# Seven block products for each branch's gates, with weight sums made by adding transfers and by VectorE

## The reference, cut to what matters

```
mod = silu(c) @ ada_w + ada_b -> shift_m, scale_m, gate_m, shift_f, scale_f, gate_f   (6 x 1024)
h = rms_norm(x) * (1 + scale_m) + shift_m
proj = h @ w_in     -> inputs of four mixers (pool, spatial gating, conv, attention), and gate_cols (256 x 4096)
branch[n] = y_n @ w_branch[n]                       n = 0..3, each (256 x 256) @ (256 x 1024)
merged = sum over n of sigmoid(gate_cols[n]) * branch[n]
x = x + gate_m * (merged @ w_out)
h2 = rms_norm(x) * (1 + scale_f) + shift_f
route each token to 6 of 64 experts; x = x + gate_f * (experts(h2) + shared(h2))
out = rms_norm(x)
```

## Time and profile before

| | us |
|---|---|
| median of three runs | 766.91 |
| the profiled execution's own time | 767.08 |
| its span, first to last instruction | 765.3 |
| TensorE busy | 724.8 (95%) |
| VectorE busy | 333.1 (44%) |
| ScalarE busy | 171.4 (22%) |
| GpSimd busy | 35.7 (5%) |
| bytes moved by DMA | 271.43 MB |

### The profile page before, as it was taken

The page is one execution under the profiler, slowest core; times in us unless marked ns, Lnnn a source line. Parts: engine busy times, 40 slices in busy tenths (PEclk is TensorE's granted clock), DMA queues, the critical chain, the costliest instruction groups (busy, mean ns, idle before and its releaser), DMA issues.

```text
span 765.3 us, 11751 instructions
## 1 busy us (share of the span) xinstructions
PE 724.8 (95%) x4678; PEld 320.0 (42%) x4678; DVE 333.1 (44%) x793; ACT 171.4 (22%) x345; POOL 35.7 (5%) x30
## 2 busy tenths in 40 slices
PE   4899999999999999999999999999999997999894
PEld 1588854444444444343343433433333342333231
DVE  1108695979743485333234332331333332322234
ACT  3213332000001333222122221221222221212113
POOL 0200001223130000000000000000000000000000
PEclk9999999999999999999999999999999999999997
DMA  9999617968668398999999999999999999999992
GB/s 341 378 352 389 199 51 275 366 213 326 252 243 361 133 382 285 394 415 419 406 400 421 421 419 417 412 421 420 420 421 420 412 417 421 420 422 420 415 402 87
DMA packets 67204, 271.43 MB, mean 355 GB/s; under 512 B 4984, under 2 KB 13312, under 8 KB 46544
## 3 DMA queue, kind: packets, MB, share of 16 engines
q1 hardware_dynamic: 65584, 264.78, 87.4%
q0 software_dynamic: 1264, 5.79, 2.0%
q10 hardware_dynamic: 304, 0.13, 0.1%
HBM read 269.62 MB, written 1.05 MB: 354 GB/s over the span
## 4 chain that ended last, share of the span: by engine, by line
PE 73%; DMA 19%; SPq 3%; DVE 2%; ACT 1%; issue 1%; POOLq 0%; ACTq 0%; DVEq 0%
PE bank L1198 71%; DMA ring<-exp_w_dram 16%; DMA ring<-w_in_dram 2%; SPq L375 2%; SPq L378 2%; PE bank L1586 1%; DMA reg<-reg 1%; PE bank L1388 0%; DVE bank L1151 0%; DVE reg L1031 0%; PE bank L1287 0%; POOLq L116 0%; ACT L650 0%; ACT h_hT L675 0%; ACT reg L549 0%
## 5 line engine op out<-in xcount | busy, mean ns | idle before, releaser
L1198 PE MATMUL bank<-ring,h_hT 128*32 128x512 f32 (+2 forms) x2368 | 373.5, 589 | 10.9 <-DMA ring<-exp_w_dram 10.8
L1198 PEld LDWEIGHTS bank<-ring,h_hT 128*32 128x32 f32 (+1 forms) x2368 | 129.3, 122 | 211.5 <-issue 190.8
L1198 PE MATMUL bank<-ring,const_misc 128*32 128x512 f32 x1008 | 116.5, 595 | 3.2 <-ACT const_misc L698 2.2
L1151 DVE TENSOR_TENSOR bank<-bank,reg 128x512 f32<-128x512 f32 x64 | 44.5, 695 | 62.2 <-PE bank L1198 62.2
L1155 DVE TENSOR_TENSOR y_part<-bank,y_part 128x512 fp32r<-128x512 f32 x64 | 44.3, 692 | 42.4 <-ACT y_part L704 21.2
L1132 DVE TENSOR_TENSOR reg<-reg,bank 128x256 f32<-128x256 f32 x32 | 13.5, 421 | 102.4 <-ACT reg L691 102.4
L691 ACT ACTIVATE reg<-bank 128x256 f32<-128x256 f32 x32 | 12.3, 385 | 204.2 <-PE bank L1198 204.2
L1198 PEld LDWEIGHTS bank<-ring,const_misc 128*32 128x32 f32 x1008 | 30.5, 109 | 64.5 <-issue 61.4
L1198 PE MATMUL bank<-ring,reg 128*128 128x512 f32 x128 | 56.1, 592 | 0.0
L1129 DVE TENSOR_REDUCE slot_gate<-bank 32x1 f32<-32x2 f32 x128 | 19.9, 156 | 70.7 <-PE bank L1198 67.7
L818 DVE SCALAR_TENSOR_TENSOR part<-ring,cact,part 128x512 f32<-128x512 f32 x56 | 47.7, 851 | 4.3 <-DVE part L818 1.6
(11 more groups left out here) (234 smaller groups left out, 430.7 us busy)
## 6 DMA issues: line engine op xcount, KB each, us to landing
ring<-exp_w_dram SPq DMA_DIRECT2D x155, 1024.0 KB, 15.1
ring<-exp_w_dram SPq DMA_DIRECT2D x67, 512.0 KB, 14.0
ring<-ada_w_dram SPq DMA_DIRECT2D x24, 1024.0 KB, 13.6
ring<-w_in_dram SPq DMA_DIRECT2D x24, 1024.0 KB, 12.1
ring<-w_branch_dram SPq DMA_DIRECT2D x4, 1024.0 KB, 13.1
ring<-w_out_dram SPq DMA_DIRECT2D x4, 1024.0 KB, 15.1
reg<-ada_bp_dram POOLq DMA_DIRECT2D x4, 512.0 KB, 7.8
ring<-shared_w_dram SPq DMA_DIRECT2D x2, 1024.0 KB, 8.1
```

What stands on the lines that cost most here:

```text
L1151: dve.tensor_tensor(bank[B_Y[hf]][:, :], bank[B_Y[hf]][:, :], gate_f[:, hf * 512:(hf + 1) * 512], ALU.mult)\
L1198: return pe.matmul(o, lhsT, rhs, start=start, stop=stop, skip_group_check=True)
```

## The change

The 1024 x 1024 block of gates is taken as 2 x 2 blocks (tokens halves A1, A2 by halves of the inner dimension; W_n in B11, B12, B21, B22 of 512 x 512), and a branch's gates are seven block products of four 128x512 matmuls each, 28 for 32. The sums of h's blocks (`token_sums`, four VectorE instructions of 128x512) are made once. The weight sums are made for each branch: two with DMAs that add to what lies at the destination (`accum_op`), issued by GpSimd (`sums_3_1`), and two on VectorE over 128x2048 (`sum_2`, `sum_4`). `w_sum` takes x's place in SBUF, so x is loaded again at the end. The results are put together by ScalarE copies and five VectorE additions a branch (`combine`).

Beside that: late ada units are now 256 rows by 1024 columns, two 128x1024 instructions each in place of four of 128x512; they have three ring slots (4, 10, 11), branch units one (5), gates two sets of four; a sum of 1024 columns lies in one of two places (`row_acc`); casts alternate between two buffers (`cast_rows`); conv taps are split 9, 14, 4 and 4 where they were 15, 4 and 12; the last `cast_out` comes before the output projection.

```diff
+    units += gates(0) + late(0, 3) + gates(1) + [("branch", 0)] + late(3, 4)
+    units += gates(2) + [("branch", 1)] + late(4, 8)
+    units += gates(3) + late(8, 10) + [("branch", 2)] + late(10, 13)
+    units += [("out", i) for i in range(4)] + late(13, 15) + [("branch", 3)] + late(15, 16)
+    return units + [("sw1", 0), ("sw3", 0)]
...
+            def sums_3_1(n):                      # GpSimd
+                if n:
+                    pool.wait_ge(S["prod_done"], N_P * (n - 1) + P_7)
+                    pool.wait_ge(S["t_done"], N_S + N_T * (n - 1) + T_2)
+                pool.dma_start(w_sum.rearrange("p (k n) -> p k n", k=4), source(("gate", 4 * n + B12))).then_inc(S["t3_in"], 16)
+                arrived(n, B11)
+                arrived(n, B12)
+                pool.dma_start(b_block(n, B12), b_block(n, B11), accum_op=ALU.add).then_inc(S["t1_in"], 16)
+                arrived(n, B22)
+                pool.wait_ge(S["t3_in"], 32 * n + 16)
+                pool.dma_start(w_sum, b_block(n, B22), accum_op=ALU.add).then_inc(S["t3_in"], 16)
...
+            pool.wait_ge(S["unit_done"], 1)
+            sums_3_1(0)
+            sums_3_1(1)
             (shared_w2, four biases and ffn_norm_g, as before)
+            sums_3_1(2)
+            cast(0) ... cast(3)
+            sums_3_1(3)
+            cast(4)
+            cast(5)
+            pool.dma_start(x_sb[:, :, :], a["x"][0]...).then_inc(S["late_in"], 16)
+            cast(6)
+            cast(7)
...
+            def sum_2(n):                         # VectorE
+                dve.wait_ge(S["t3_in"], 32 * (n + 1))
+                dve.wait_ge(S["t1_in"], 16 * (n + 1))
+                dve.wait_ge(S["prod_done"], N_P * n + P_1)
+                dve.tensor_tensor(b_block(n, B11), w_sum, b_block(n, B11), ALU.add).then_inc(S["t_done"], 1)
+            def sum_4(n):
+                dve.wait_ge(S["prod_done"], N_P * n + P_2)
+                dve.wait_ge(S["t_done"], N_S + N_T * n + T_2)
+                dve.tensor_tensor(b_block(n, B21), b_block(n, B21), b_block(n, B11), ALU.add).then_inc(S["t_done"], 1)
...
+            for n in range(1, NB):                # VectorE, n = 1 and 2; n = 3 has four late units and more cast_outs
+                cast_out, accumulate(first), sum_2(n), combine(n, C_11), cast_out, sum_4(n)
+                accumulate(first + 1), combine(n, C_T), accumulate(first + 2), combine(n, C_22)
+                accumulate(first + 3), combine(n, C_12), accumulate(first + 4), combine(n, C_21)
+                merge(n, 0) ... merge(n, 3)
...
-                gate_columns(n, 0) ... gate_columns(n, 3)     # TensorE, 8 matmuls each
+                product_1(n), product_2(n), product_7(n), product_5(n), product_6(n), product_3(n), product_4(n)   # 4 each
+            product_7 waits for t3_in 32 * (n + 1), product_5 for t1_in, product_6 for sum_2, product_3 for combine C_T,
+            product_4 for sum_4
```

More of the change, by code:

```diff
@@ L65 @@
 N_EARLY = 8
-ADA_AT = [0, 2, 1, 3, 4, 5, 8, 9, 6, 7, 10, 11]
-CONV_FIRST = 15
+ADA_AT = [0, 2, 1, 3]
+LATE_ROWS = [2, 4, 3, 5]
+CONV_EARLY, CONV_FIRST, CONV_MORE = 9, 23, 27
 BLOCK = [(0, 0), (0, 1), (1, 1), (1, 0)]
-TILES = [(0, 0), (0, 1), (1, 1), (1, 0)]
-def unit_plan():
[L75 to L81, removed]
@@ L84, with gates, late @@
-UNITS = unit_plan()
[L85 to L89, removed]
+B11, B12, B22, B21 = range(4)
+T_2, T_4 = 1, 2
+P_1, P_2, P_7, P_5, P_6, P_3, P_4 = 1, 2, 3, 4, 5, 6, 7
+C_11, C_T, C_22, C_12, C_21 = 1, 2, 3, 4, 5
+N_S, N_T, N_P, N_C, N_A = 4, 2, 7, 5, 3
+def unit_plan():
+    def gates(n):
+        return [("gate", 4 * n + b) for b in (B12, B11, B22, B21)]
+    def late(first, last):
+        return [("ada", N_EARLY + i) for i in range(first, last)]
+    units = [("ada", i) for i in range(N_EARLY)] + [("mix", i) for i in range(8)]
+    units += gates(0) + late(0, 3) + gates(1) + [("branch", 0)] + late(3, 4)
[3 more added lines that the diff above has]
+    return units + [("sw1", 0), ("sw3", 0)]
@@ new lines, in slot_of @@
+def slot_of(u):
+    kind, i = u
+    if kind == "gate":
+        return [6, 0][i // 4 % 2] + [1, 0, 2, 3][i % 4]
+    if kind == "ada" and i >= N_EARLY:
+        return [4, 10, 11][(i - N_EARLY) % 3]
+    return {"ada": [1, 2, 3, 5, 6, 7, 8, 9], "mix": [4, 10, 11, 0, 1, 2, 3, 5], "branch": [5] * NB, "out": [6, 7, 8, 9],
+            "sw1": [10], "sw3": [11]}[kind][i]
+UNITS = unit_plan()
+SLOT = {u: slot_of(u) for u in UNITS}
+LAST, BEFORE, FILLS = {}, {}, {}
+for _u in UNITS:
+    FILLS[_u] = 0
+    if SLOT[_u] in LAST:
+        BEFORE[_u] = LAST[SLOT[_u]]
+        FILLS[_u] = FILLS[BEFORE[_u]] + 1
+    LAST[SLOT[_u]] = _u
@@ L773, in _, with conv_taps @@
                               sig_c[:, :, :], ALU.mult).then_inc(unit_read[1], 1)
+            def conv_taps(first, last):
+                for i in range(first, last):
+                    for j in range(2):
+                        w = pr("conv_w", j * TAPS + i, j * TAPS + i + 1)
+                        src = glu[:, j, i:i + T]
+                        if i:
+                            dve.wait_ge(S["conv_done"], 2 * i + j - 1)
+                            ins = dve.scalar_tensor_tensor(out=conv[:, j, :], in0=src, scalar=w, in1=conv[:, j, :],
+                                                           op0=ALU.mult, op1=ALU.add)
+                        else:
+                            ins = dve.tensor_scalar(conv[:, j, :], src, w, pr("conv_b", j, j + 1), ALU.mult, ALU.add)
+                        ins.then_inc(S["conv_done"], 1)
@@ new lines, in accumulate @@
+            def accumulate(i):
+                v, q = i // 4, i % 4
+                u = ("ada", N_EARLY + i)
+                w = unit(u).rearrange("p (k n) -> p k n", k=2)
+                acc = row_acc[v % 2]
+                dve.wait_ge(landed[SLOT[u]], 16 * (FILLS[u] + 1))
+                if q == 0 and v >= 2:
+                    dve.wait_ge(S["cast_done"], 2 * (v - 1))
+                for k in range(2):
+                    at = cact[:, 2 * q + k:2 * q + k + 1]
+                    if q or k:
+                        dve.wait_ge(S["acc_step"], 2 * i + k)
+                        ins = dve.scalar_tensor_tensor(out=acc, in0=w[:, k, :], scalar=at, in1=acc, op0=ALU.mult, op1=ALU.add)
+                    else:
+                        ins = dve.tensor_scalar(acc, w[:, k, :], at, None, ALU.mult)
+                    ins.then_inc(S["acc_step"], 1)
+                dve.wait_ge(S["acc_step"], 2 * i + 2)
+                dve.sem_inc(S["acc_done"], 1)
@@ L943, in _ @@
             conv_norm_1()
+            combine(0, C_12)
+            combine(0, C_21)
             conv_norm_2()
@@ L953, in _ @@
             merge(0, 3)
[L954 removed]
+            dve.wait_ge(S["conv_sig"], 2)
             dve.tensor_tensor(y[:, 2, :, :], conv[:, :, :], sq_c[:, :, :], ALU.mult).then_inc(S["conv_y"], 1)
[L956 to L975 removed]
+            accumulate(1)
+            for n in range(1, NB):
+                first = [1, 2, 7, 12][n]
+                if n > 1:
+                    cast_out([0, 0, 0, 2][n])
+                if n < 3:
+                    accumulate(first)
+                sum_2(n)
+                combine(n, C_11)
+                if n > 1:
+                    cast_out([0, 0, 1, 3][n])
+                sum_4(n)
+                if n < 3:
+                    accumulate(first + 1)
+                else:
+                    accumulate(first)
+                combine(n, C_T)
+                if n < 3:
+                    accumulate(first + 2)
+                else:
+                    accumulate(first + 1)
+                    cast_out(4)
+                combine(n, C_22)
+                if n < 3:
+                    accumulate(first + 3)
+                else:
+                    accumulate(first + 2)
+                combine(n, C_12)
+                if n < 3:
+                    accumulate(first + 4)
+                else:
+                    accumulate(first + 3)
+                combine(n, C_21)
+                for q in range(4):
+                    merge(n, q)
+            for m in (5, 6, 7):
+                cast_out(m)
             def residual_2(k):
@@ L1118, in _ @@
             shared_product(1)
-            cast_out(7)
             def body(use, final=False):
```

313 lines of the change are left out of this document (191 added, 122 removed).

## The result

The changed kernel takes 783.83 us (median of 4 runs, 782.69 to 785.79) beside 766.90 us for the kernel before: a ratio of 1.022, 95% interval 1.0205 to 1.0235, or 16.9 us more. The forecast was 762.4 us, faster than before, with a range up to 778 us; the change made the kernel slower, by more than that.

What follows compares the result with a forecast made beforehand. TensorE bounds before 268 us, loads after 300. TensorE saves 13.7 us, VectorE leaves 9.2, the DMA engines allow 7.3, less 2.6 for a landing: 4.7 us gained, 767.08 - 4.7 = 762.4 us. Range 756.5 to 778.

Steps and rivals of the forecast that it cites:

- TensorE's part: Gates of each branch: four matmuls of 0.858 us fewer, 3.43 us a branch, 13.7 us over four, the most possible.
- Branch 0 stalls nowhere: Branch 0: VectorE's added sums, combines and taps fit into holes, so branch 1 begins at 130.9 us for 134.4.
- VectorE's part: Branches 1 to 3: TensorE waits about 1 us in branch 2, 3.5 in branch 3; 4.5 of 13.7 lost, 9.2 left.
- One for one to the end: Mixing stage to end: its gain or loss shifts the first slot release, all expert loads and the end equally.
- The DMA's part: Branches 1 to 3, 109 to 237.6 us: DMA engines allow 7.3 us of gain, 4.7 after an unhidden landing.
- I take 3.75, between one pass and two: Price of one 1 MB adding transfer in us of DMA time; six from 109 us on make 22.5 us.
- the upper bound of two passes: An adding transfer must read both operands, so from above it costs 5.0 us of DMA time for 1 MB.
- The reason I gave against two passes: Reads and writes of two queues may overlap, and a load leaves SBUF's read side idle.
- the allowance: DMA time from 109 to 237.6 us: 34.8 idle + 5 - 10 for loads - 22.5 for adding transfers = 7.3 us.
- one landing: Branches 1 to 3: 2.6 us beyond the bytes for a load of the sums, taken as not hidden.
- Branch 0's transfers: Branch 0's two adding transfers, placed in the stage from 80 to 109 us with its DMA idle share of 0.39.
- The slower rival: Adding transfers hold up product 7 and sum_2 of branches 2 and 3; 772.5 us at 5.0 us each; chance 0.32.

Runs made afterwards that it cites:

- Experiment 7: Seven products in branches 0 and 3 only of the changed kernel, eight in 1 and 2: 762.71 us, ratio 0.9945 to the kernel before.
- experiment 10: Changed kernel with seven products in branches 0 and 1 only, shared_w2 and bias loads issued after the fifth late unit: 760.93 us, ratio 0.992 to before.
- experiment 9: Changed kernel, all eight adding transfers kept, with shared_w2 and the five bias rows issued after branch 2's sums: 779.18 us, ratio 1.0164 to before.
- experiment 12: Changed kernel, all transfers kept; in branch 1 VectorE accumulates three late units after the four merges, not between combines: 778.46 us, ratio 1.0152 to before.
- experiment 3: Changed kernel with adding transfers cut to 16 of 2048 columns and w_sum loads to 16 of 512: 757.76 us, ratio 0.9892 to before.
- Experiment 1: Changed kernel with both adding transfers of each branch made plain copies of the same 1 MB: 768.65 us, ratio 1.0019 to before.

## Why the prediction was wrong, by its steps

- **TensorE's part: right.** A branch's gates take 24.04 us, as forecast. Branch 0 stalls nowhere and branch 1 begins at 130.81.
- **VectorE's part: right in size.** A sum over 128x2048 takes 2.28 us (forecast 2.3), a late unit 2.60 and its gap of 0.23 (2.85). With no traffic for the sums the kernel takes 757.76 us, 9.3 under before; the term left 9.2. That the two agree to 0.1 us is in part luck: TensorE waits 2.8 us for VectorE there (1.4 in branch 2 and 1.4 at the end of branch 3), where I had laid out about 1 and 3.5.
- **One for one to the end: right.** From the first transposes to the end of the span it is 529.6 us before, and 528.7 to 530.5 in all twelve experiments. Only the profiled run of the change has 532.3; its cause is open, and its median is 2.0 us under that run.
- **The DMA's part: the step that failed**, in its price and in its form. "I take 3.75, between one pass and two" was the mis-sized term: 4.75 us were measured, within 0.25 of the upper bound of two passes. The reason I gave against two passes, that reads and writes may overlap, made nothing cheaper here: an adding transfer took 2.0 times a copy. The Trainium skill (Collectives: The Full Stack, section The bandwidth ceiling: the fold count and why AG ≠ RS ≠ AR) has a reducing transfer, there of a collective, at half the rate of a copy. The runs agree for these transfers, 4.75 for 2.35 us. I had cited it and given the rival that rests on it only 0.32.
- With 4.75 the allowance is 34.8 + 5 - 10 - 28.5 = 1.3 us, and less one landing, 1.3 us slower: 768.4. That is 15 us from the result, so the price alone is not the cause. **The form was wrong**: I pooled the idle time from 109 to 237.6 us as if any transfer could use any of it. In the changed kernel two branches' sums (from 109 us on and from the end of product 7 of branch 1) and 3.6 MB for biases and the shared expert are issued before 160 us, where late units are due; the later idle time is of no use to them. Experiment 7 shows the same transfers costing 2.3 us in branch 3 for 9.0 in branch 1, experiment 10 shows that they make TensorE wait nowhere in branch 1 once 4.6 MB of plain loads stand behind, and experiment 9 that 3.6 MB of these cost 4.7 us.
- **Branch 0's transfers** were put in the wrong stage. I had them from 80 to 109 us with its share of 0.39; GpSimd issued them at 66.76 and 69.45; from 60 to 80 us the share is 1.06, and it was 1.05 before the change. They pushed SP's loads back into the stage from 80 on, whose share rose to 0.83. There was room, and it cost nothing.
- **The slower rival had the price and not the place.** It looked for products and `sum_2` waiting for `t3_in`. They never waited. What came late were SP's loads, which share the engines with the adding transfers, and VectorE's list carried it to TensorE (experiment 12). A late unit is issued when VectorE is done with the one in its slot, and that left 11.5 us to the first of them; I had no term for this. I had the row for it, a late unit just in time before, and priced one landing at 2.6 us; it was 14.29 and 6.07.

How the 16.9 us come about, as differences of medians: seven products, sums' traffic aside, -9.3 (experiment 3 to before); four plain loads +2.5; eight copies +8.4; the additions in them +15.2. (The kernel before was timed anew with each group of runs, 766.90 and 767.02 here, so the four add up to 16.8.) Copies and additions are 38 us of DMA time by the queue's share, of which 23.6 reached the end; the rest found idle engines.

One part of the stall's cost is not the wait itself. TensorE's granted clock was 1.00 until the stall. In the 10 us after 160, in which TensorE did nothing, and in the next 10 its mean was 0.59 and 0.56, so it stood mostly at the lower of its two levels, 1.2 GHz for 2.4:

```profile
160.00:170.00 10.00, 0.00 (x0) 0.00 (x0) 8.88 (x5) 0.63 (x1) 7.20 (x2) 0.59 1.01 347
170.00:180.00 10.00, 5.12 (x8) 2.27 (x9) 7.65 (x11) 1.26 (x2) 0.00 (x0) 0.56 1.05 388
```

The branch tile behind the wait then took 5.67 us for 3.60, and 6.08 in branch 2: some 4.5 us in all, on top of waits of 22.8 us. Experiment 1 separates the two. Its waits for `merge` are far shorter, 3.41 and 4.12 us, yet it pays about as much in the tiles behind them, 2.97 and 1.80 us:

```profile
162.09 6.57 PE L1379 MATMUL bank<-ring,reg 128*128 128x512 f32 x8 [3.41 <-DVE reg L1084]
...
200.93 5.40 PE L1379 MATMUL bank<-ring,reg 128*128 128x512 f32 x8 [4.12 <-DVE reg L1084]
```

So the 15.2 us between it and the change are the waiting itself (15.3 us less of it); the clock costs 4.5 to 4.8 us in both, and nothing in experiment 10, where TensorE never waits. In experiment 3 a wait of 1.20 us left the instructions behind it at their full pace.

## What to carry to other kernels

Price a transfer that adds as two of its size until it is measured, and sum DMA time by stage and deadline, not over a phase: idle engines 60 us later do not help a load that is due now. When a busy queue gets more traffic, look for the victim among all loads on the engines: take for each the time from the release of its slot to the moment at which it is wanted, and follow a late one through the in-order list of the engine that reads it. An idea that loses when it is used in all four branches may still pay where there is room: seven products in two of four branches, with the traffic nobody awaits moved back, gained 0.8%.

## What the runs showed of the hardware

- A transfer from SBUF to SBUF that adds 1 MB takes 4.75 us of the 16 engines' time, a copy 2.35, a load of `w_sum` (32.6 - 21.9) / 4 = 2.7. With adding transfers in flight the engines are busy at 1.04 and deliver 249 GB/s, with copies 398 at 1.02.
- The share of DMA busy time can stay at 1.0 while the rate falls by a third. Read both columns.
- A GpSimd addition of 128x2048 takes 4.5 to 6.6 us and holds a VectorE instruction with two operands in SBUF for its whole length (4.72 us for 0.47); instructions with one operand in PSUM took 0.68 us beside it, as ever. A cast of 3.31 us took only 1.85 us from VectorE.
- Waits of TensorE of 3.41 to 16.44 us behind `merge` (experiments 1 and 9 and the change) were each followed by a branch tile that took 1.8 to 3.0 us more, with a granted clock of 0.56 to 0.83 in the 10 us around; a wait of 1.20 us (experiment 3) was followed by instructions at full pace and a clock of 1.00.
